# Hybrid mixer and FFN layer on one core: column strips for the adaLN products, an earlier mixer, summed channels, earlier splits, and the two-tile block moved from first to second place

## The reference, cut to what matters

```
mod = silu(c) @ w_ada + b_ada                     # c: 1 + 8 rows of 1024, w_ada: 1024 x 6144
sh1, sc1, gt1, sh2, sc2, gt2 = split(mod, 6)
h = rmsnorm(x, g_pre_mix) * (1 + sc1) + sh1
xa, xb, xc = split(h @ w_in)                      # 1024 x 2176
ya = window means (2, 4, 8, 16) of xa minus xa, times w_pool, times s_pool
yb = silu(layernorm(conv31(a * sigmoid(g)) + b_dw))   # 384 channels; mean and variance over channels
yc = b * conv3(c * h)                             # 384 channels
x = x + gt1 * rmsnorm(concat(ya, yb, yc) @ w_out, g_post_mix)
h = rmsnorm(x, g_pre_ffn) * (1 + sc2) + sh2
x = x + gt2 * rmsnorm((silu(h @ w_gate) * (h @ w_up)) @ w_down, g_post_ffn)   # D_FF = 2816
```

## Time and profile before

| what | us |
|---|---|
| median of 3 runs | 2366.36 |
| lowest, highest | 2365.51, 2370.28 |
| profiled execution | 2368.96 |
| its span | 2367.2 |
| TensorE busy in it | 2318.4 |
| VectorE, ScalarE busy | 1340.9, 1029.7 |

### The profile page before, as it was taken

One profiled execution on the slowest core, in us unless ns is written; L12 is line 12 of the kernel. 1 busy time (PEld: TensorE's weight loads), 2 busy tenths in 40 slices (PEclk: granted clock), 3 DMA queues, 4 the chain that ended last, 5 costly groups with the idle time before them and its releaser, 6 DMA issues.

```text
span 2367.2 us, 30248 instructions
## 1 busy us (share of the span) xinstructions
PE 2318.4 (98%) x12452; PEld 2094.2 (88%) x12452; DVE 1340.9 (57%) x1917; ACT 1029.7 (43%) x1433; POOL 40.2 (2%) x82
## 2 busy tenths in 40 slices
PE   8999998999999999999999999999999998999998
PEld 2848897897999898899999899989889996899987
DVE  1775796569744367844357773436784433443343
ACT  2435554545353444435353435444443424433232
POOL 0000000000000000000000000000000000000000
PEclk9999999999999999999999999999999999999999
DMA  8664463344533353353344344335334432534332
GB/s 303 229 214 153 144 228 131 132 173 173 174 143 126 124 178 129 139 186 123 127 137 166 125 175 146 125 125 178 125 125 176 120 130 100 178 134 170 131 127 89
DMA packets 101743, 361.64 MB, mean 153 GB/s; under 512 B 12259, under 2 KB 14435, under 8 KB 101604
## 3 DMA queue, kind: packets, MB, share of 16 engines
q1 hardware_dynamic: 101606, 359.70, 43.3%
HBM read 340.73 MB, written 18.93 MB: 152 GB/s over the span
## 4 chain that ended last, share of the span: by engine, by line
PE 93%; DVE 4%; DMA 2%; ACT 1%; issue 1%; SPq 0%; POOL 0%; POOLq 0%; DVEq 0%; ACTq 0%
PE ps L474 92%; DVE wlo L1083 1%; PE ps L516 1%; DVE pr L1210 1%; DMA raw<-in_w_ada 1%; DMA raw<-in_w_gu 0%; DVE g_lo L1132 0%; DMA gate<-in_gpost 0%; DMA raw<-in_w_mix 0%; DVE h_lo L1125 0%; DVE xr L1156 0%; ACT whi L726 0%; ACT junk L768 0%; ACT junk L745 0%; DVE xt L1146 0%
## 5 line engine op out<-in xcount | busy, mean ns | idle before, releaser
L474 PE MATMUL ps<-h_hi,whi 128*128 128x384 f32 (+1 forms) x2928 | 958.5, 327 | 4.0 <-DVE wlo L1083 3.6
L474 PE MATMUL ps<-h_hi,wlo 128*128 128x384 f32 (+1 forms) x2928 | 954.2, 326 | 0.0
L474 PE MATMUL ps<-h_lo,whi 128*128 128x384 f32 (+1 forms) x2928 | 954.1, 326 | 0.0
L1083 DVE TENSOR_TENSOR wlo<-raw,whi 128x1024 fp32r<-128x1024 f32 x546 | 664.3, 1222 | 502.2 <-ACT whi L726 491.1
L726 ACT ACTIVATE whi<-raw 128x1024 fp32r<-128x1024 f32 x546 | 576.0, 1057 | 789.9 <-DMA raw<-in_w_gu 531.4
L474 PEld LDWEIGHTS ps<-h_hi,whi 128*128 128x128 f32 x2928 | 552.7, 189 | 10.5 <-issue 6.4
L474 PEld LDWEIGHTS ps<-h_lo,whi 128*128 128x128 f32 x2928 | 552.6, 189 | 1.9 <-issue 0.3
L474 PEld LDWEIGHTS ps<-h_hi,wlo 128*128 128x128 f32 x2928 | 552.4, 189 | 0.0
L1210 DVE SCALAR_TENSOR_TENSOR pr<-u,col,pr 128x384 f32<-128x384 f32 x450 | 260.2, 614 | 1.2
L474 PE MATMUL ps<-whi,g_hi 128*128 128x512 f32 x748 | 236.1, 397 | 12.0 <-DVE g_lo L1132 10.4
L474 PE MATMUL ps<-whi,g_lo 128*128 128x512 f32 x748 | 231.4, 390 | 0.0
(11 more groups left out here) (110 smaller groups left out, 1160.8 us busy)
## 6 DMA issues: line engine op xcount, KB each, us to landing
raw<-in_w_gu SPq DMA_DIRECT2D x264, 512.0 KB, 3.2
raw<-in_w_mix SPq DMA_DIRECT2D x150, 512.0 KB, 3.3
raw<-in_w_dn SPq DMA_DIRECT2D x132, 512.0 KB, 3.2
raw<-in_w_ada SPq DMA_DIRECT2D x48, 512.0 KB, 4.3
xt<-in_x_all SPq DMA_DIRECT2D x17, 512.0 KB, 6.2
xr<-in_x_all SPq DMA_DIRECT2D x17, 512.0 KB, 5.8
xr<-x_all SPq DMA_DIRECT2D x17, 512.0 KB, 6.0
x_all<-xr SPq DMA_DIRECT2D x5, 1536.0 KB, 7.3
```

Of the source, the lines that this page charges most:

```text
L474: return nc.tensor.matmul(out, lhsT, rhs, start=start, stop=stop, skip_group_check=True)
L1083: tt(wlo[:, s, :], raw[:, s, :], whi[:, s, :].bitcast(F32), ALU.subtract).then_inc(w_lo, 1)
```

## The change

NT becomes [3, 2, 3, 3, 3, 3]. Four adaLN units at a time are multiplied in four strips of 32 columns of the array, each strip writing its own 32 partitions of the same bank (ada_units); mod then has 106 rows, and ada_columns and gate_rows add the strips up by constants with ones in four places (E_FOLD, E_SELP, E_SELS). All 24 first units come before the projection of block 0. mixing(1) begins before normalise(0) and goes on in the output product of block 0, with taps written to the `early` tile until the last; glu order is the same for all blocks. The wait for the gpost load moves from before the projection of block 0 to the first gate. For b > 0 VectorE adds the three channel tiles of z and of the squares, and TensorE multiplies each sum once by ones. In the last chunk hidden 2 is split in the output product too, and x_square moves one step ahead.

```diff
-NT = [2, 3, 3, 3, 3, 3]
+NT = [3, 2, 3, 3, 3, 3]
-C_PAD = 32
-MOD_K = ROWS + 1
+C_PAD, STRIPS = 32, 4
+BIAS = C_PAD * (STRIPS - 1) + ROWS
+MOD_K = BIAS + 1
-STREAM = [("ada", n) for n in range(ADA_HEAD - 2)]
+STREAM = [("ada", n) for n in range(ADA_HEAD)]
 for j_ in range(NIN):
     STREAM.append(("in", 0, j_))
-    if j_ < 2:
-        STREAM.append(("ada", ADA_HEAD - 2 + j_))
-IN_FIRST, IN_ADA = 4, 3
-IN_PROJ = [None, (6, 3), (5, 3), (5, 3), (5, 3), (5, 3)]
+IN_FIRST, IN_ADA, IN_OUT = 4, 4, 2
+IN_PROJ = [None, (6, 4), (5, 3), (5, 3), (5, 3), (5, 3)]
-IN_GATE_UP = [6, 5, 5, 5, 5]
+IN_GATE_UP = [8, 5, 5, 5, 5]
...
-            def ada_unit(i):
+            def ada_units(q):
...
                 for h in range(2):
-                    w = slice(512 * h, 512 * h + 512)
-                    last = mm(ps[0:C_PAD, 2 + 2 * pair + h, :], c_s[:, k, :], raw[:, n % RING, w], k == 0, k == KD - 1)
-                last.then_inc(w_used, 1)
+                    for i in range(STRIPS):
+                        n, strip = UNIT["ada", STRIPS * q + i], C_PAD * i
+                        if h == 0:
+                            pe.wait_ge(w_landed[n % RING], landed(n))
+                        last = nc.tensor.matmul(ps[strip:strip + C_PAD, 2 + 2 * ADA_PAIR[g] + h, :], c_s[:, k0 + i, :],
+                                                raw[:, n % RING, 512 * h:512 * h + 512], start=k0 == 0,
+                                                stop=k0 + STRIPS == KD, tile_position=(0, strip), skip_group_check=True)
+                        if h:
+                            last.then_inc(w_used, 1)
...
+                elif b and i == 2:
+                    pe.wait_ge(z_summed, b)
+                    last = mm(out, ones, pslot("g", 2)[:, 0:w], True, True)
+                elif b:
+                    pe.wait_ge(zsq_summed, b)
+                    last = mm(out, ones, pslot("b", 0)[:, 0:w], True, True)
...
-            for i in range(ADA_HEAD, ADA_ALL):
-                ada_unit(i)
-                if i == ADA_HEAD + 1:
+            for q in range(ADA_HEAD // STRIPS, ADA_ALL // STRIPS):
+                ada_units(q)
+                if q == 6:
                     pe.wait_ge(evac_done, evac_count(0, NIN - 1))
-                if i < 5 * KD and i % 2:
-                    transposes(1, (i - ADA_HEAD) // 2)
+                if q < 10:
+                    transposes(1, 2 * (q - 6))
+                    transposes(1, 2 * (q - 6) + 1)
...
-                    elif c and k >= NMIX - 2:
-                        hidden_high(c - 1, k - (NMIX - 2))
+                    elif c and k >= NMIX - G_RING:
+                        hidden_high(c - 1, k - (NMIX - G_RING))
...
-                        if c + 1 == NB and k == 1:
+                        if c + 1 == NB and k == 0:
                             for t in range(NT[c]):
                                 x_square(norm("F", c), t)
...
+            def add_three(b, kind, into, done):
+
+                w = NT[b] * P
+                x0, x1, x2 = (pslot(kind, j)[:, 0:w] for j in range(NCONV))
+                after(own.step(tt(into, x0, x1, ALU.add)))
+                tt(into, into, x2, ALU.add).then_inc(done, 1)
+
+            def sum_z(b):
+                dve.wait_ge(z_ready, NCONV * (b + 1))
+                dve.wait_ge(evac_done, evac_count(b, NIN - 1))
+                add_three(b, "a", pslot("g", 2)[:, 0:NT[b] * P], z_summed)
+
+            def sum_squares(b):
+                dve.wait_ge(zsq_ready, NCONV * (b + 1))
+                add_three(b, "b", pslot("b", 0)[:, 0:NT[b] * P], zsq_summed)
...
             dve.wait_ge(state_landed, 48)
-            dve.wait_ge(gpost_landed, 32)
             mixer = mixing(0)
...
+            mixer = mixing(1)
+            advance(mixer, 5)
             normalise(0)
...
                 for k in range(NMIX):
                     ahead("out", c, k)
+                    if c == 0:
+                        advance(mixer, IN_OUT)
...
                         elif m == s - 1:
                             finish(mixer)
+                            sum_z(c + 1)
                         elif m == s + 1:
                             centre(c + 1)
                             y_rest(c + 1, 0, NY1)
+                        elif m == s + 2:
+                            sum_squares(c + 1)
```

More of the change, by code:

```diff
@@ L373, in _ @@
             sp.dma_start(col[:, :], cols).then_inc(const_landed, 16)
-            sp.dma_start(mod[ROWS:MOD_K, :, :], b_ada[:, 0:3]).then_inc(bias_landed[0], 16)
+            sp.dma_start(mod[BIAS:MOD_K, :, :], b_ada[:, 0:3]).then_inc(bias_landed[0], 16)
             sp.dma_start(con_a[:, :], consts_a).then_inc(const_landed, 16)
-            for n in range(RING, ADA_HEAD - 2):
+            for n in range(RING, ADA_HEAD):
                 load("ada", n)
@@ L632, in _ @@
             pe.wait_ge(c_ready, 1)
-            for i in range(ADA_SHIFT):
-                ada_unit(i)
+            for q in range(ADA_SHIFT // STRIPS):
+                ada_units(q)
             pe.wait_ge(const_landed, 48)
@@ L1202, in tap @@
                 def tap(j, k, at):
-                    z = tokens("a", j)
+                    z = src = raw_in("a", j)
+                    if first:
+                        z = src = runs(z)
+                    elif k == TAPS - 1:
+                        z = tokens("a", j)
+                        if b == 1:
+                            dve.wait_ge(w_used, UNIT["out", 0, NMIX - 1] + 1)
                     wk = col[:, Q_WDW + j * TAPS + k:Q_WDW + j * TAPS + k + 1]
@@ L1300, in mixing @@
                 at0 = yield from glu(0)
-                if b == 1:
-                    at1 = yield from glu(1)
-                    at2 = yield from glu(2)
-                if b:
-                    dve.wait_ge(w_used, UNIT["out", b - 1, NMIX - 1] + 1)
                 for k in range(HEAD):
@@ L1308, in mixing @@
                     yield
-                if b != 1:
-                    at1 = yield from glu(1)
+                at1 = yield from glu(1)
                 for k in range(HEAD, TAPS):
@@ L1315, in mixing @@
                     yield
-                if b != 1:
-                    at2 = yield from glu(2)
+                at2 = yield from glu(2)
                 for k in range(TAPS - HEAD, TAPS):
@@ L1423, in _ @@
             ahead("in", 1, 3)
-            gate(3, 6)
             y_rest(0, NY1, NMIX)
             ahead("in", 1, 4)
+            gate(3, 6)
             ahead("in", 1, 5)
@@ L1434, in _ @@
                             h_rest(norm("M", c + 1), ch)
-                    elif c and k >= NMIX - 2:
-                        hidden_low(c - 1, k - (NMIX - 2))
-                mixer = mixing(c + 1) if c + 1 < NB else None
+                    elif c and k >= NMIX - G_RING:
+                        hidden_low(c - 1, k - (NMIX - G_RING))
+                if c:
+                    mixer = mixing(c + 1) if c + 1 < NB else None
                 if c + 1 < NB:
@@ L1444, in _ @@
                         first, count = IN_PROJ[c + 1]
-                        if j >= first:
+                        if j >= first and j != j0 + 1:
                             advance(mixer, count)
@@ L1525 @@
     consts_a[:, E_ONES:E_ONES + P] = 1
-    consts_a[0, E_SELP:E_SELP + P] = 1
-    for s in range(SEQS):
-        consts_a[1 + s, E_SELS + s * STEPS:E_SELS + (s + 1) * STEPS] = 1
-    consts_a[ROWS, E_SELP:E_CNT] = 1
+    for i in range(STRIPS):
+        consts_a[C_PAD * i, E_SELP:E_SELP + P] = 1
+        for s in range(SEQS):
+            consts_a[C_PAD * i + 1 + s, E_SELS + s * STEPS:E_SELS + (s + 1) * STEPS] = 1
+        consts_a[C_PAD * i + np.arange(ROWS), E_FOLD + np.arange(ROWS)] = 1
+    consts_a[BIAS, E_SELP:E_CNT] = 1
+    consts_a[BIAS, E_FOLD + ROWS] = 1
     for g, w in enumerate(WINDOWS):
```

81 lines of the change are left out of this document (37 added, 44 removed).

## The result

The changed kernel takes 2352.49 us (median of 4 runs, 2351.77 to 2354.01), the kernel before 2366.18 beside it on the same chip: a ratio of 0.9939 [0.9922, 0.9957], some 14 us faster. Forecast were 2322 us, 44 less, with a range of 2308 to 2341. The sign is right, a third of the gain is there, and the time lies above the range. The profiled execution has a span of 2351.0 us, against 2367.2.

The account below looks back on a forecast made before the run. TensorE was taken to set the time in chunks c = 2 to 4, with losses elsewhere. The terms summed to -44.1 us from 2368.96 profiled, giving 2324.9, less 2.6 to the median: 2322 us, range 2308 to 2341.

Parts of the forecast that it names:

- eleven units of block 1: Block 1's projection after block 0's output product: eleven units shorter by 1.28 us each with two tiles, -14.1 us.
- Term 1: Head and adaLN stage, with strips and a three-tile block 0: project(1) starts at 181.7 against 169.7, +12 us.
- Term 7: Last chunk: hidden 2 split earlier removes the hole, next unit starts at 1996 instead of 2007.4, -11.4 us.
- Term 4: Chunk c = 1, holding the two-tile block's gate-up: 1.4 us wait for g_f, channel sums -2.6; in all -43.0 us.
- Term 3: Gate-up of c = 0: 185.4 us for 146.4, so +39.0, made of +56.5 for the tile and -17.5 gain.
- Term 2: First six units of block 1: -7.7 us with two tiles, about 2.5 taken back by variance, gates and splits; -5.
- the output product: Output product of block 0, one tile larger: +10.9 us.
- c = 2: Chunk c = 2, where down of the two-tile block comes: -28.8 us with its sums (term 5).
- the channel sums of the three-tile blocks: Chunks c = 3 and 4: four fewer float32 matmuls save 2.6 us per block, -5.2 us (term 6).
- Strips serial: Rival for the adaLN stage: strips serial or at halved clock, groups of 7.1 to 8 us, 2332 us; chance 0.14.
- VectorE as the bound: Rival: VectorE limits block 1's two-tile gate-up and projection, 1 us lost per m and unit, 2341 us; chance 0.10.

Follow-up runs that it names:

- e1: From the changed kernel, chunk 0's store of x1 moved behind the loads of gate-up m = 1: 2344.41 us, ratio 0.9898 to the kernel before.
- e6: From e1, two mixer steps instead of four per unit in block 1's projection: 2340.64 us, ratio 0.9876 to the kernel before.
- e2: The changed kernel with the old block sizes, NT = [2, 3, 3, 3, 3, 3], all else kept: 2331.63 us, ratio 0.9842 to the kernel before.
- e3: The kernel before with only the blocks swapped, NT = [3, 2, 3, 3, 3, 3]: 2378.13 us, ratio 1.0039 to the kernel before.
- e5: From the changed kernel, six mixer steps per unit instead of four in block 0's projection: 2351.28 us, ratio 0.9925 to the kernel before.
- e7: From e2, ScalarE's copy of the last adaLN group placed ahead of the weight splits: 2329.05 us, ratio 0.9829 to the kernel before.
- e11: From e9, next chunk's statistics two units later in gate-up, STATS_AT = [14, 10, 8, 8, 8]: 2329.25 us, ratio 0.9835 to the kernel before.
- e4: From the changed kernel, all four adaLN units of a group in the same 32 columns, no strips: 2380.2 us, ratio 1.0044 to the kernel before.
- e9: From e6, with the edits of e5 and e7 added, the blocks still swapped: 2333.52 us, ratio 0.9852 to the kernel before.
- e8: From e2, the last chunk's splits and squares of x as in the kernel before: 2338.84 us, ratio 0.987 to the kernel before.
- e10: From e7, five mixer steps instead of four per unit in block 1's projection: 2330.81 us, ratio 0.9847 to the kernel before.
- e12: From e7, the gpost load moved from unit 4 to unit 9 of block 0's projection: 2328.84 us, ratio 0.9832 to the kernel before.

## Why the prediction was wrong, and where it was right

**The step that failed** is the costing of the swap: "Moving a tile from one block to another costs TensorE nothing over the whole run; what it changes is what stands beside it", and then "eleven units of block 1, 11 x 1.28: -14.1" with nothing set beside them. The first clause stands; the second was not followed through. Beside those eleven units stands `store` in SP's list, whose wait for the residual grew by a tile while the units it holds up shrank by a third. What the runs showed in place of a free move is TensorE's wait of 8.55 us behind that store, and behind it VectorE too late for norm F 0. The store's wait was there before and was hidden under units of 4.15 us; I hadn't listed it. SP's waits in the kernel before, 220 to 260 us:

```profile
SPq L363 <- DVE xr L1156: 7.6, 1, 7.6
```

13.2 of the 27.9 missing us are in that row of the table. e1 returns 9.0 there (8.7 by the spans) and e6 another 4.2 (2.0 by the spans, 3.8 by the medians).

**One gain for two edits.** "+56.5 is the tile and -17.5 the gain" was near for all parts together (15.3 measured), but e2 has 12.1 of it without the swap and e3 11.6 with nothing but the swap. The sum suffered little from that; the view of which edit pays did, and hid that the swap here brings nothing that the other parts don't.

**Term 1** was near (1.2 off), with strips faster and the transposing products slower than assumed. I had taken 4.0 us per group, with the second record of a product held back behind the first; it is 1.92, so nothing of the kind shows, but the loads' pace of about 6 us was the step that mattered, and it held (5.7 to 6.6). I named a pooling instruction as the releaser of the sums. It is ScalarE's copy of mod, with pooling right behind (e5, e7).

**Term 7** was mis-sized: -6.6 for -11.4. The hole did go from 10.08 to 5.30 us and the next hole was forecast at 4 to 5. But I measured the gain from a stage mark at 2007.4 in the earlier trace rows as though the fourth down unit started there; after 1991.99 TensorE ran without a break in the kernel before, so only the difference of the two holes and of the slow rows behind them could be won.

**Term 4**: 4.2 off. The wait for g_f was within the 1.4 that I had left (0.9). The channel sums were not: "have 4.15 us before sums are due" holds for a three-tile block, and here 0.5 + 1.5 + 0.9 us stood against 2.87. That is a wait of 2.2 us and 1.7 of lower clock (e11). **Term 3** is 2.2 off: behind the two holes its matmuls start every 0.32 us, instead of every 0.173, from 298.50 to 304.05, at a granted clock of 0.51, which costs 2.5 us where I had put 1. **Term 2** is 2.0 off, its chain of gates and splits taking back 4.7 of the 7.7 and not 2.5.

**Right:** the output product, c = 2 and the channel sums of the three-tile blocks (2.5 per block) to 0.2 us, the start of the first projection (58.0 for 57.5), no wait for the mixer in gate-up of c = 0, and the strips running side by side. Here the row of the 189 ns weight load under a 173 ns pitch had pointed the right way. The Trainium skill (TensorE: Matmul & The Clock Gate, Part 3, The mechanism) has in one of its sentences that weight loads overlap running matmuls only where row groups differ. The strips here share all rows, and 16 records in 1.92 us for 7.05 do not agree with a serial reading of it.

**The rivals.** Strips serial was priced at +10 and is +28 (e4): I had VectorE's end as a floor that would hide the rest, but the gate rows too come 12.0 us later, and VectorE's work hangs on them. VectorE as the bound came true in part (e6), and not at a microsecond per unit in all.

## What to carry to other kernels

When blocks change size, go through the list of the engine that issues transfers and ask of each wait in it how long it holds the loads behind it, in the new units of time: a store that waits 9.4 us is nearly free behind units of 4.15 us (e2), and one that waits 9.9 costs 9 behind units of 2.87. An edit that puts work on another engine is priced anew in the shortest stage that has to cover it. Two edits that relieve the same wait are priced together, once. And where a stall goes, look at what was catching up under it before the gain is booked: removing the store's wait gave 8.7 us of 13, and the rest needed the next one removed too.

## What the hardware showed that was not expected

Eight float32 products of 128 x 32 with 512 columns, two in each of four column strips, take 1.92 us for their 16 records, against 7.05 in one strip: nearly the full factor of four. Against that, a float32 matmul with few columns is dear. The products that turn mod to columns, in the change (a timeline row, then the weight loads of both such stages, minimum, median and maximum in ns):

```profile
163.97 3.82 PE L475 MATMUL ps<-con_a,mod 106*128 106x10 f32 x32 [1.63 <-ACT mod L882]
```

```profile
L475 PEld LDWEIGHTS ps<-con_a,mod x64: 186/192/296, 40.7 to 167.4; 106*128 106x128 f32 x64
```

32 records in 3.82 us are 0.12 us each for ten columns, and a float32 product has two of them: 0.24 for a block of 128 channels. The kernel before turned the same 16 blocks by transposes in 1.15 us, 0.07 each.

A small wait of TensorE can cost as much again behind it. In the six traces where the wait for the sum of squares of a two-tile stage is 2.0 to 2.3 us (the change, e1, e4, e5, e6, e9), the granted clock of the 7 us behind it is 0.76 to 0.78; in the six where it is 1.4 to 1.6 (e2, e7, e8, e10, e11, e12), it is 1.00. No run lies between, and none varies the wait alone.
